# A two-layer expert network: down gathers ahead of up gathers, twelve up slots at the end, and mixing or gates of three tiles beside them

## The reference, cut to what matters

```python
def peer_block(xb, w_q, sub_keys, expert_u, expert_v):
    q = (xb @ w_q).reshape(T, PEER_HEADS, 2, PEER_HALF)        # 8 heads
    s = einsum('thpd,hpkd->thpk', q, sub_keys)                 # 2 x 128 keys
    sv, si = lax.top_k(s, 16)
    cand = sums of all 16 x 16 pairs; top_s, pos = lax.top_k(cand, 16)
    eidx = the 16 experts (of 16384) of the best pairs
    gate = softmax(top_s)
    u = take(expert_u, eidx)                                   # 16 rows of 1024 per token and head
    act = gelu(einsum('thkd,td->thk', u, xb))
    v = take(expert_v, eidx)
    return einsum('thk,thkd->td', gate * act, v)
```

```python
proj = xn @ w_in           # b_gate, c_gate, v_conv, u_pool: 512 columns each
z = c_gate * v;  y = conv_w[0]*z[t-1] + conv_w[1]*z[t] + conv_w[2]*z[t+1];  y_conv = b_gate * y
y_pool = (mean of u over windows of 2, 4, 8, 16 tokens - u) @ pool_w * pool_scale
h = h + concat([y_conv, y_pool]) @ w_o
```

## Time and profile before

| what | value |
|---|---|
| median of 3 runs | 3505.99 us (3505.01 to 3507.85) |
| the profiled execution's own time | 3508.9 us |
| its span | 3506.9 us |
| busy: PE, DVE, ACT, POOL | 1952.4, 2033.8, 686.0, 2069.9 us |
| moved by DMA | 1168 MB, of it 1074 MB by POOL's gathers |
| chain that ended last, by engine | DMA 31%, POOL 25%, PE 23%, issue 10%, DVE 4% |

### The profile page before, as it was taken

How to read it: one execution, slowest core, us unless ns; L and a number is a source line. 1 busy time by engine, 2 the same in 40 slices (tenths; PEclk the granted TensorE clock), 3 DMA queues, 4 the chain that set the end, 5 groups by cost and what they waited for, 6 DMA issues and landing times.

```text
span 3506.9 us, 30318 instructions
## 1 busy us (share of the span) xinstructions
PE 1952.4 (56%) x9949; PEld 948.9 (27%) x9949; DVE 2033.8 (58%) x4967; ACT 686.0 (20%) x1897; POOL 2069.9 (59%) x2098
## 2 busy tenths in 40 slices
PE   8998996444444444444446984443444444444457
PEld 3554653112221221211212452121211211211212
DVE  1244427666666666666762248666666766666642
ACT  3021223121112111122211022111111112121212
POOL 1313215777677767776773017777677677766660
PEclk9999798776666576666567997666666767666678
DMA  6213147999999999999998149999999999999992
GB/s 231 75 69 108 48 156 278 409 409 409 390 409 409 409 386 409 409 409 399 409 409 300 68 188 403 409 409 409 390 409 409 389 407 409 409 408 409 408 365 81
DMA packets 334192, 1168.08 MB, mean 333 GB/s; under 512 B 36027, under 2 KB 39381, under 8 KB 331733
## 3 DMA queue, kind: packets, MB, share of 16 engines
q0 software_dynamic: 294912, 1073.87, 77.4%
q1 hardware_dynamic: 39124, 92.27, 7.1%
HBM read 1163.92 MB, written 2.10 MB: 332 GB/s over the span
## 4 chain that ended last, share of the span: by engine, by line
DMA 31%; POOL 25%; PE 23%; issue 10%; DVE 4%; ACT 1%; POOLq 0%; DVEq 0%; ACTq 0%
PE banks L689 16%; POOL ring L653 15%; POOL scr L644 10%; DMA ring<-in_expert_v,idx_v 9%; DMA ring<-in_peer_up,idx_v 8%; DMA scr<-in_peer_down,idx 8%; DMA scr<-in_expert_u,idx 6%; PE banks L1044 6%; DVE scr L1906 2%; ACT hT L1211 0%; DVE X L1923 0%; POOL ring L620 0%; DMA ring<-in_w_mod 0%; DVE const L1748 0%; ACT hT L1225 0%
## 5 line engine op out<-in xcount | busy, mean ns | idle before, releaser
L1906 DVE CUSTOM_DVE_ANT_0 scr<-scr,banks 128x1024 f32<-128x1024 f32 x1024 | 1241.0, 1220 | 809.6 <-DMA scr<-in_expert_u,idx 397.3
L1044 PE MATMUL banks<-ring 128*32 128x512 f32 x4096 | 829.7, 953 | 1356.3 <-DMA ring<-in_expert_v,idx_v 678.1
L644 POOL DMA_INDIRECT scr<-in_expert_u,idx x512 | 481.4, 940 | 336.7 <-DVE idx L1882 159.2
L1044 PEld LDWEIGHTS banks<-ring 128*32 128x32 f32 x4096 | 163.9, 148 | 1770.0 <-issue 1762.7
L653 POOL DMA_INDIRECT ring<-in_expert_v,idx_v x512 | 485.7, 949 | 230.7 <-issue 140.3
L653 POOL DMA_INDIRECT ring<-in_peer_up,idx_v x512 | 486.4, 950 | 221.4 <-issue 143.2
L644 POOL DMA_INDIRECT scr<-in_peer_down,idx x512 | 482.7, 943 | 210.8 <-issue 127.5
L689 PE MATMUL banks<-ring,scr 128*128 128x128 f32 (+1 forms) x2112 | 311.6, 313 | 73.7 <-DVE X L1923 65.7
L689 PEld LDWEIGHTS banks<-ring,scr 128*128 128x128 f32 x2112 | 284.6, 217 | 92.2 <-DVE X L1923 66.4
L617 POOL TENSOR_TENSOR ring<-ring,silu 128x4096 f32<-128x4096 f32 x8 | 56.2, 7022 | 313.1 <-DMA ring<-in_w_mod 313.1
L689 PE MATMUL banks<-ring,hT 128*128 128x512 f32 x512 | 224.7, 597 | 1.8 <-DVE hT L1792 1.0
(11 more groups left out here) (211 smaller groups left out, 1970.9 us busy)
## 6 DMA issues: line engine op xcount, KB each, us to landing
ring<-in_w_mod SPq DMA_DIRECT2D x12, 2048.0 KB, 8.5
ring<-in_w_in SPq DMA_DIRECT2D x7, 2048.0 KB, 13.0
scr<-in_peer_w_q SPq DMA_DIRECT2D x1, 8192.0 KB, 27.9
scr<-in_peer_down,idx POOLq DMA_INDIRECT x512, 12.0
ring<-in_peer_up,idx_v POOLq DMA_INDIRECT x512, 11.9
scr<-in_w_q SPq DMA_DIRECT2D x1, 8192.0 KB, 23.5
scr<-in_expert_u,idx POOLq DMA_INDIRECT x512, 12.0
ring<-in_expert_v,idx_v POOLq DMA_INDIRECT x512, 11.9
```

Of the source, the lines that this page charges most:

```text
L644: nc.gpsimd.indirect_dma_start(u_rows[:, k % SLOTS, :], None, table_u, bass.IndirectOffsetOnAxis(idx[:, n % IDX_SLOTS, k:k + 1], 0)).then_ ...
L1044: last = nc.tensor.matmul(psum[2 + c][32 * g:32 * g + 32, :], spread[:, n % 2, k, :], v_rows[k % SLOTS][:, c * CW:(c + 1) * CW], start=(h ...
L1906: V.tensor_tensor_reduce(u_rows[:, k % SLOTS, :], u_rows[:, k % SLOTS, :], xn, 1.0, 0.0, ALU.mult, ALU.add, dots[:, n % 2, k:k + 1]).then_ ...
```

## The change

Five parts, in both layers unless said otherwise.

1. **Order of the gathers.** Behind up batch b POOL issues down rows until `clock(b+1)` = 24 + 16(b+1)/3 are out: five or six per batch instead of four. All 512 down rows are out with batch 91. PE and ACT no longer loop over heads but over batches; `heads_at(batch, offset)` gives each step of a head its place by the same clock. Packed weights and up indices now keep 16 heads (V_HEADS) instead of 2 and 4.
2. **Twelve up slots from batch 94 on** (WIDE_FROM), with the third set in the first down slots and in `const` (layer 0) or in four down slots (layer 1). POOL waits ahead of batch 94 until every down row is used and every head routed.
3. **Mixing of tiles 0 to 2 beside up rows** (layer 0). Columns of tokens 0 to 383 for all 16 groups stand behind batches 101 to 116, the products behind the windows behind 117 to 120, the norms of tiles 0 and 1 behind 94 and 95, tile 2's behind 100. DVE's convolution and window sums for tokens 0 to 375 stand behind its last dot product. Tile 3 (`ccL`, `cvL`, `puL`, `cbL`, `pyL`) is done as layer 1 opens.
4. **Gates of tiles 0 to 2 beside up rows** (layer 1), with their products and final norms, behind batches 96 to 113.
5. **New order as a layer opens.** DVE routes heads 0 and 1 ahead of any dot product, and takes those in two groups of eight; PE has scores of head 2 ahead of the last projection, and norms of tiles 1 to 3 at the end. SP loads the second half of `w_in_2` beside the gathers, `w_o_2` and `sub_keys_2` when the last up row is used, and `w_q_2` in four pieces.

```diff
+V_HEADS = 16
+N_ROWS = N_HEADS * TOPK
+N_BATCH = N_ROWS // 4
+WIDE_FROM = 94
+def clock(batch):
+    return U_LEAD + 16 * batch // 3
+def u_issued(batch):
+    return min(N_ROWS, clock(batch))
+def v_set(batch):
+    return batch % 2 if batch < WIDE_FROM else (2, 0, 1)[(batch - WIDE_FROM) % 3]
+def v_last(batch):
+    return batch - (2 if batch < WIDE_FROM else 3)
+def heads_at(batch, offset):
+    before = clock(batch - 1) if batch > 0 else U_LEAD - 1
+    return [n for n in range(N_HEADS) if before < TOPK * n + offset <= clock(batch)]
...
+        v_more = [[at(scr, 0, D), at(scr, D, D), at(const, C_COS, D), at(const, C_AHEAD, D)],
+                  [at(scr, D * k, D) for k in range(QUADS)]]
...
-                for first in range(0, N_HEADS * TOPK, QUADS):
-                    for i in range(first, first + QUADS):
+                for b in range(N_BATCH):
+                    if b == WIDE_FROM:
+                        pool.wait_ge(u_used, (layer + 1) * N_ROWS + SLOTS)
+                        pool.wait_ge(s_done, (layer + 1) * N_HEADS)
+                        pool.wait_ge(routed, (layer + 1) * N_HEADS + 2)
+                    for i in range(QUADS * b, QUADS * b + QUADS):
                         v_gather(i // TOPK, i % TOPK)
-                    for i in range(first + U_LEAD, min(first + U_LEAD + QUADS, N_HEADS * TOPK)):
+                    for i in range(u_issued(b), u_issued(b + 1)):
                         u_gather(i // TOPK, i % TOPK)
...
+                for batch in range(N_BATCH):
+                    for m in heads_at(batch, 0):
+                        if m % PH == 0 and m > 0:
+                            pe.wait_ge(u_used, (n0 + m) * TOPK + SLOTS)
+                            block_rows()
+                    for m in heads_at(batch, TOPK + 4):
+                        move_weights(m)
+                    for m in heads_at(batch, SLOTS - TOPK):
+                        move_idx(m)
+                    for m in heads_at(batch, SLOTS - 2 * TOPK):
+                        scores_q(m)
+                    for m in heads_at(batch, SLOTS - 2 * TOPK + 4):
+                        scores_s(m)
+                    add_up(batch)
+                    if batch in beside:
+                        beside[batch]()
...
+            beside = {94: lambda: tile_rows("gm", 0), 95: lambda: tile_rows("gm", 1), 100: lambda: tile_rows("gm", 2),
+                      101: first_cols, 109: first_pool_cols}
             for j in range(4):
...
+                if j > 0:
+                    beside[101 + 2 * j] = lambda j=j: early_cols("cc", j, 0)
+                    beside[109 + j] = lambda j=j: early_cols("pu", j, 2 * CW)
+                beside[102 + 2 * j] = lambda j=j: early_cols("cv", j, CW)
+                beside[113 + j] = lambda j=j: early_cols("cb", j, 3 * CW)
+                beside[117 + j] = lambda j=j: early_pool(j)
+            peer(0, start_first, beside)
...
+            beside = {94: lambda: tile_rows("gp", 0), 95: lambda: tile_rows("gp", 1), 96: lambda: p_cols(0), 97: lambda: p_cols(1),
+                      98: lambda: gate(0, 0), 99: lambda: gate(0, 1), 100: lambda: products(0), 101: third_rows,
+                      103: lambda: gate(1, 0), 105: lambda: gate(1, 1), 107: lambda: products(1),
+                      109: lambda: gate(2, 0), 111: lambda: gate(2, 1), 113: lambda: products(2)}
...
+            sp.wait_ge(v_used, N_ROWS + V_CREDIT)
+            for col in (0, CW):
+                load_chunk(chunk_number("w_o_2", col))
+            load_chunk(chunk_number("keys_2"))
...
+            def start_second(route, route_keys, softmax, dot_products, pack_idx):
...
+                add_projection(1, "wo2", 0)
+                tile_stats("gf", 0)
+                late_conv()
+                tile_out("gf", 0, gains, None)
+                late_pool()
+                late_gate()
+                route(0)
+                route_keys(0)
+                softmax(0)
+                pack_idx(0)
+                route(1)
+                route_keys(1)
+                dve.wait_ge(xn_ready, TT + 1)
+                dot_products(0, range(SLOTS))
```

897 lines of the change are left out of this document (524 added, 373 removed).

## The result

The changed kernel takes **3461.7 us** (median of four runs, 3456.4 to 3467.2); the kernel before took 3505.5 beside it. The ratio is 0.987, with a 95% interval from 0.986 to 0.988. The forecast was 3410 with a range from 3378 to 3465: the sign is right and the range holds the time, but of the 99 us forecast only 44 came. The profiled execution took 3461.0 us, its span is 3459.0.

The account below looks back on a forecast made before the run. The prediction took the kernel as bound by transfers for most of its time, the rest being two holes and a front; terms of -6, +19, -68, -19 and -25 us sum to -99, from 3508.9 to 3410 us, range 3378 to 3465.

Parts of the forecast that it names:

- The tail: From layer 1's last add-up to the end of the span: 36 us against 61.1, minus 25 us.
- The saving between the layers: From layer 0's last add-up to layer 1's first head 1 dot product: 138 us against 205.8, minus 68.
- The opening: Start of a layer up to head 1's first dot product; in layer 0 579.5 us against 585.9, minus 6.
- S: Cut point at a layer's first dot product of head 1, forecast at 579.5 us and, in layer 1, 2,059.5.
- E to S: From the end of layer 0's last add-up to layer 1's first head 1 dot product: 138 us, bounds 118 and 165.
- The term for the plateau itself: Loss at tile boundaries while both kinds of rows run: 6 us in layer 0, bounds 0 and 12.
- S to T: From head 1's first dot product to the last down row consumed: 1127 us in layer 0, 1121 in layer 1.
- T to E of layer 1: Up rows alone, last down row consumed to last add-up, gates beside them: 191 us.
- T to E of layer 0: Up rows alone, last down row consumed to last add-up: 215 us, 27 of them paid for hiding the mixing.
- rival 3: PE runs at the lower clock beside up rows alone: 3588 us, slower by 82; chance 4%.
- Rival 2: POOL, held by down rows waiting for DVE, paces the mixed stretches: 3465 us; chance 12%.
- Rival 4: ScalarE or DVE returns a bank or spread matrix late, so the mixing does not hide: 3492 us; chance 4%.

Follow-up runs that it names:

- e5: Changed kernel, layer openings reordered: tile 2's projection before tile 1's statistics, five head 1 dot products before head 2's routing, head 1's indices moved earlier; 3432.2 us.
- e12: Changed kernel with only one move of e5: head 1's first five dot products ahead of its softmax, packed indices and head 2's routing; 3442.9 us.
- e16: Changed kernel with one of eight matmuls in each of the six gate products beside layer 1's up rows; 3452.4 us.
- e10: Changed kernel with the third set of up slots opened at batch 93 instead of 94, each row waiting for its own slot; 3453.8 us.
- e11: Changed kernel with one of eight matmuls in each of the 16 mixing product groups beside layer 0's up rows; 3432.1 us.
- e9: Changed kernel with each VectorE dot product reading 512 of its 1,024 columns, gathers as large as before; 3452.4 us.
- e6: Changed kernel with e5's reordering, the 16 product groups spread over batches 99 to 122, and layer 1's output weights loaded earlier; 3405.9 us.

## Why the prediction was right and wrong

**The removed work came out as forecast.** The tail was 34.7 instead of 36, the first gather of layer 1 77.9 behind the last add-up instead of 78. Sixteen products ran at 7.2 us a batch. The saving between the layers (205.8 to 148.2) and at the end (61.1 to 34.7) is 84 of the 93 us forecast for the two.

**The steps that failed** are terms of the sum, in this order of size.

*The opening, S in both layers and what follows it (some 30 of the 51 us).* The prediction let POOL refill the queue at S as the kernel before does, and cut there. But the change puts head 1's routing ahead of dot products 0 to 7 and leaves head 2's routing ahead of head 1's first dot product; before, the last up and down rows were issued just ahead of S (402 GB/s) and now the queue has been empty for five us (10 GB/s). The first 20 us of the stretch at 253 GB/s cost 20 x (1 - 253/409) = 7.6 us that stood in no term. The prediction also took the waits between TensorE and VectorE at zero (5.0 and 4.3 us in layer 0) and the last projection at full clock (16.32 instead of 14.00 us). The first gather of layer 1 came where the forecast had it, so all 10.2 us over from E to S are this opening. e5 gets back 29.5 us by order alone, e12 18.8 of them with one move. The term for the plateau itself was right. In layer 0's S to T, cut in slices of 20 us, those below 403 GB/s cost 7.6 us in the first, 6.6 in seven others together, where 6 were taken, and 2.3 in the last 17 us ahead of T (356 GB/s); the sum of 16.5 is 10.5 over the 6, which is the whole of that row. The bytes are 874 gathers' worth, where 876 were taken.

*T to E of layer 1 (12.8 us).* "Six gate products of 7.0 us ... T + 191" let the gates hide nearly whole. e16 shows 9.5 us for their sum, e10 6.9 for the end of the down rows. Each is known to some 5 us only, as this piece took 199.4 to 204.8 us with nothing of it edited, so how the 12.8 us divide stays open.

*T to E of layer 0 (7.8 us).* The prediction gave 27 us for the products and e11 measures 34.0; the first of them ended at T + 61 instead of T + 55. "The wide slots open only when all down rows are used, so batch 94 lands near T + 10": the first wait came one batch earlier, batch 93 waiting with eight slots for batch 91's add-up (7.7 us), and 94 landed at T + 16. Batch 96, which also waits for tile 2's output, came at T + 30 instead of T + 25. e10 takes the wait ahead of batch 93 away and gains 3.0 us here, so it is a part of the 7.8.

*Readings.* The 6.2 us for a gather in an emptied queue is the median of twelve issued 1.24 us apart; the first of them, alone in the queue, landed in 4.3 us (its row in the DMA view of the kernel before), still above the 3.2 us that the prediction works out beside it. And the rows that rival 3 is argued against with show an add-up of 1.92 us ahead of the pair of mixing products (10.59 us), not one of 3.64. In the same trace the pair at 1909.09 stands behind an add-up of 3.64 us and took 11.62 us, so a slow start costs such a pair 1 us and not its whole length again.

**The rivals.** Rival 2 (12%) gave 3465 and the time is 3462, but for another reason: e9 takes 30% of VectorE's load away and gains 3.8 and 2.3 us in S to T. A number that fits is not its mechanism. Rival 3 did not come: TensorE's granted clock is 1.00 over the hundred us of products, and each runs at 5.43 us. The Trainium skill (TensorE: Matmul & The Clock Gate, HAM oscillation — how this bites in real kernels) has groups of matmuls behind waits for transfers start slow; the trace agrees for a lone add-up (3.64 us) and not where a product of 5.4 us stands behind each. Rival 4 came only on the other kind of chip, in a place that nobody named: the weights of a head, not the mixing.

## What to carry to other kernels

Cut two kernels at the same instruction only where the queue is in the same state on both sides: compare the transfer rate in the few microseconds ahead of the cut first. When work is hidden beside transfers, add up the covering engine's time per unit and space it so that each group of units stays under the transfers' time; here sixteen products in a row cost 34 us and the same sixteen behind two batches of three some 10 (e6, which has other edits too). And ahead of a long in-order job (a routing of 5 us) look for short ones that free a slot for another queue: five dot products moved in each layer gave 19 us.
